# Local attention: the bias goes from two TensorE products to one VectorE addition, and the scores from a float32 product of 64 rows to two fp32r products of 128 rows

## What is computed

```python
    dist = jnp.arange(WINDOW)[:, None] + WINDOW - jnp.arange(2 * WINDOW)[None, :]
    swa_bias = rel_bias[t5_bucket(jnp.maximum(dist, 0))].transpose(2, 0, 1)
...
    s = jnp.einsum('bnqhgd,bnjhd->bnhgqj', qb, kb).astype(jnp.float32) * d ** -0.5
    s = s + bias.astype(jnp.float32).reshape(Hkv, G, W, 2 * W)
...
    s = jnp.where(valid[None, :, None, None], s, -jnp.inf)
    sink = jnp.broadcast_to(sinks.astype(jnp.float32).reshape(1, 1, Hkv, G, 1, 1),
                            s.shape[:-1] + (1,))
    p = jax.nn.softmax(jnp.concatenate([s, sink], axis=-1), axis=-1)[..., :-1]
    out = jnp.einsum('bnhgqj,bnjhd->bnqhgd', p.astype(v.dtype), vb)
```

## Time and profile before

| | |
|---|---|
| median of 3 runs | 1845.63 us (1845.04 to 1845.82) |
| the profiled execution | 1847.51 us, span 1845.7 us |
| mean granted TensorE clock of the span | 0.98 of full |
| TensorE busy | 1772.8 us, 96% |
| VectorE, ScalarE, GpSimd busy | 51%, 45%, 52% |
| DMA | 162.15 MB, mean 88 GB/s |

### The profile page before, as it was taken

One profiled execution on the slowest core, in us unless ns is written; L12 is line 12 of the kernel. 1 busy time (PEld: TensorE's weight loads), 2 busy tenths in 40 slices (PEclk: granted clock), 3 DMA queues, 4 the chain that ended last, 5 costly groups with the idle time before them and its releaser, 6 DMA issues. The chain is left out here.

```text
span 1845.7 us, 27645 instructions
## 1 busy us (share of the span) xinstructions
PE 1772.8 (96%) x10494; PEld 1551.0 (84%) x10494; DVE 941.2 (51%) x1590; ACT 825.5 (45%) x1649; POOL 954.7 (52%) x697
## 2 busy tenths in 40 slices
PE   6999999999998999999979999999899989999998
PEld 4998777778887998899868988888788779989996
DVE  2444233345446772475048337995323288717842
ACT  4223434323334652455236327885434356515643
POOL 2453322224443775577436417994463247747862
PEclk8999999999999999999989988999999989999999
DMA  6232121113352223233324312011251223333341
GB/s 226 80 92 58 44 60 41 55 44 97 89 182 80 87 97 115 80 115 109 120 66 127 114 34 69 2 36 58 92 160 60 78 69 92 109 109 92 93 137 46
DMA packets 222900, 162.15 MB, mean 88 GB/s; under 512 B 9768, under 2 KB 197296, under 8 KB 222768
## 3 DMA queue, kind: packets, MB, share of 16 engines
q1 hardware_dynamic: 221712, 159.32, 28.1%
q10 hardware_dynamic: 1056, 1.06, 0.2%
HBM read 156.15 MB, written 2.11 MB: 86 GB/s over the span
## 5 line engine op out<-in xcount | busy, mean ns | idle before, releaser
L350 POOL TENSOR_TENSOR w_low<-ring,w_high 128x1024 fp32r<-128x1024 f32 (+2 forms) x223 | 484.2, 2175 | 639.5 <-ACT w_high L342 639.3
L363 PE MATMUL psum<-hT,w_high 128*128 128x512 f32 (+1 forms) x1072 | 378.2, 353 | 9.9 <-PEq L185 6.4
L342 ACT ACTIVATE w_high<-ring 128x1024 fp32r<-128x1024 f32 (+2 forms) x223 | 212.2, 955 | 383.4 <-PE psum L365 383.4
L364 PE MATMUL psum<-hL,w_high 128*128 128x512 f32 (+1 forms) x1072 | 371.0, 346 | 0.0
L365 PE MATMUL psum<-hT,w_low 128*128 128x512 f32 (+1 forms) x1072 | 370.7, 346 | 0.0
L363 PEld LDWEIGHTS psum<-hT,w_high 128*128 128x128 f32 x1072 | 206.7, 193 | 38.3 <-issue 11.8
L365 PEld LDWEIGHTS psum<-hT,w_low 128*128 128x128 f32 x1072 | 206.1, 192 | 24.9
L364 PEld LDWEIGHTS psum<-hL,w_high 128*128 128x128 f32 x1072 | 206.8, 193 | 21.6
L1711 POOL TENSOR_TENSOR w_low<-ffn_sums,w_high 128x512 fp32r<-128x512 f32 x120 | 169.3, 1425 | 50.4 <-ACT w_high L1706 50.0
L1711 POOL TENSOR_TENSOR w_low<-ring,w_high 128x512 fp32r<-128x512 f32 x120 | 155.4, 1298 | 60.8 <-ACT w_high L1706 54.3
L363 PE MATMUL psum<-ffn_th,w_high 128*128 128x256 f32 x640 | 181.6, 284 | 5.0 <-DVE ffn_g L1945 3.4
(11 more groups left out here) (418 smaller groups left out, 3766.1 us busy)
## 6 DMA issues: line engine op xcount, KB each, us to landing
ring<-in_w_in SPq DMA_DIRECT2D x58, 512.0 KB, 3.4
ring<-in_ffn_w_up SPq DMA_DIRECT2D x44, 512.0 KB, 3.7
ring<-in_w_gate SPq DMA_DIRECT2D x22, 512.0 KB, 3.7
ring<-in_w_up SPq DMA_DIRECT2D x22, 512.0 KB, 4.7
ring<-in_w_down SPq DMA_DIRECT2D x20, 512.0 KB, 3.7
ring<-in_ffn_w_down SPq DMA_DIRECT2D x20, 512.0 KB, 3.8
ring<-in_nsa_w_in SPq DMA_DIRECT2D x18, 512.0 KB, 3.5
ring<-in_ca_wkv SPq DMA_DIRECT2D x16, 512.0 KB, 3.6
```

Of the source, the lines that this page charges most:

```text
L342: nc.scalar.activation(tile_view(w_high, n, SPLIT), tile_view(ring, n, RING), ACT.Copy).then_inc(w_hi, 1)
L350: nc.gpsimd.tensor_tensor(tile_view(w_low, n, SPLIT), tile_view(ring, n, RING), tile_view(w_high, n, SPLIT), ALU.subtract).then_inc(w_lo, 1)
L363: nc.tensor.matmul(ps, lhsT=sh, rhs=mh, start=first, stop=False)
L364: nc.tensor.matmul(ps, lhsT=sh, rhs=ml_, start=False, stop=False)
```

## The change

The bias is no longer multiplied on TensorE. Its row of 384 is made reversed by the constants; it comes back as `bias_back`, and VectorE copies it once with its columns turned over into `bias`, float32. In each step of the local attention VectorE copies the two heads' sinks into the last column of the pair's slots in `sprob`, waits for the scores, adds PSUM and bias into `sprob`, and takes the maximum from there. ScalarE's exponential reads and writes `sprob`.

For the scores, each query head has a tile `wq[h]` of 128 rows: its high part in the 64 rows of its key head, its low part in the other 64. For each key head `wk[g]` has the high part in both halves and `wkl[g]` the low part in both. Two fp32r products of 128 rows give (high + low) x high and (high + low) x low. The tiles `wq`, `wk` and `wkl` are written from the transposes in PSUM: high parts by ScalarE, low parts by VectorE, each piece 64 partitions x 512. `qkT` keeps four tiles. `put` has one buffer in place of two, and the reversed identity is gone from the constants. Other hunks, not shown, move tiles to other addresses and rename semaphores.

```diff
@@ -111,9 +110,9 @@
         if 0 <= dist[u] < 128:
-            c[bucket[u], C_OH + u] = 1
+            c[bucket[u], C_OH + 383 - u] = 1
         else:
-            c[BUCKETS, C_OH + u] = NEG
+            c[BUCKETS, C_OH + 383 - u] = NEG
     return np.concatenate([c, r], axis=1)
...
@@ -762,31 +764,36 @@
         norm_gain = at("anorm_gain", [P, D], 8192)
-        qkT = at("qkT", [P, 9, S], 18432)
+        qkT = at("qkT", [P, 4, S], 18432)
         sqr = at("sqr", [P, 54, HD], 18432)
...
-        raw = at("raw", [P, SWA_H, 256], 57344)
         rows = at("rows", [P, 2, S], 65536, F32R)
-        mcol = at("mcol", [P, 2, NT, ML_H], 69632)
-        toep = [at(f"toep{i}", [P, SWA_H, 258], 69760 + 8256 * i, F32R) for i in range(2)]
-        sinks = at("sinks", [P, SWA_H], 104704)
-        yswa = at("yswa", [P, NT, 512], 86272)
-        sprob = at("sprob", [P, 4, 258], 12288)
-        sprobT = at("sprobT", [P, 4, 256], 94464, F32R)
-        sprobL = at("sprobL", [P, 4, 256], 98560, F32R)
-        put = at("put", [P, 2, 2, P], 102656)
+        bias = at("bias", [P, SWA_H, 256], 69632)
+        bias_back = at("bias_back", [P, SWA_H, 256], 77824)
+        wq_at = [26624 + 2048 * i for i in range(5)] + [77824 + 2048 * i for i in range(3)]
+        wq = [at(f"wq{h}", [P, S], wq_at[h], F32R) for h in range(SWA_H)]
+        wk = [at(f"wk{g}", [P, S], (83968, 102400)[g], F32R) for g in range(2)]
+        wkl = [nc.alloc_sbuf_tensor_at(f"wkl{g}", [P, S], F32R, offset=x_at + (6 + g) * 4 * S) for g in range(2)]
+        yswa = at("yswa", [P, NT, 512], 86016)
+        sprob = at("sprob", [P, 4, 258], -32)
+        sprobT = at("sprobT", [P, 4, 256], 94208, F32R)
+        sprobL = at("sprobL", [P, 4, 256], 98304, F32R)
+        put = at("put", [P, 2, P], 104448)
         yfox = at("yfox", [P, NT, 256], 45056)
...
@@ -823,15 +830,13 @@
                 for h in (2 * hp, 2 * hp + 1):
-                    g, i = h // 4, h % 4
+                    g = h // 4
                     k0 = max(t - 1, 0)
                     nk = (t + 1 - k0) * P
-                    rows_g = slice(HD * g, HD * g + HD)
                     units.append({
                         "width": nk + 1,
-                        "scores": [(0, nk + 2, anti_r, toep[0][:, h, 256 - nk:258]),
-                                   (0, nk + 2, anti_r, toep[1][:, h, 256 - nk:258]),
-                                   (0, nk, qkT[rows_g, 4 + i, q_tile(t)], qkT[rows_g, 8, k0 * P:k0 * P + nk])],
+                        "scores": [(0, nk, wq[h][:, q_tile(t)], wk[g][:, k0 * P:k0 * P + nk]),
+                                   (0, nk, wq[h][:, q_tile(t)], wkl[g][:, k0 * P:k0 * P + nk])],
                         "keys": [(j * P, vswa[:, k0 + j, g, :]) for j in range(nk // P)]})
...
@@ -973,6 +978,13 @@
                 pe.wait_ge(out_a, NT * (c + 1) - sum(n_v[:c + 1]))
+        def wait_qk_out(pe, i):
+            if i >= 4:
+                pe.wait_ge(qk_v, i - 1)
+            else:
+                pe.wait_ge(qk_v if i % 2 == 0 else qk_a, i // 2 + 1)
 
...
@@ -1029,7 +1041,7 @@
                 if i >= 3:
-                    pe.wait_ge(qk_v if (i - 3) % 2 == 0 else qk_a, (i - 3) // 2 + 1)
+                    wait_qk_out(pe, i - 3)
                 for t in range(NT):
...
@@ -1230,6 +1242,18 @@
                 scaled(False, qkT[:, i, :], bank[5 + i % 3], qk_gain(i)).then_inc(qk_a, 1)
+            def window_high(i):
+                a.wait_ge(turned_qk, i + 1)
+                src, gain = bank[5 + i % 3], qk_gain(i)
+                for g in range(2):
+                    if i < 8:
+                        nc.scalar.activation(wq[4 * g + i - 4][part(g), :], src[part(g), :], ACT.Copy,
+                                             scale=gain[part(g), :]).then_inc(w_high_qk, 1)
+                    else:
+                        for e in range(2):
+                            nc.scalar.activation(wk[g][part(e), :], src[part(g), :], ACT.Copy,
+                                                 scale=gain[part(g), :]).then_inc(w_high_qk, 1)
 
...
@@ -1244,9 +1268,12 @@
             qk_out(3)
-            qk_out(5)
+            window_high(4)
+            window_high(5)
             split_high(a, feat0 + 4 + SPLIT)
-            qk_out(7)
+            window_high(6)
+            window_high(7)
+            window_high(8)
             feature_out(5)
...
@@ -1300,7 +1327,8 @@
                         a.wait_ge(turned, v_ - 3)
-                    nc.scalar.activation(pairs[s]["prob"][:, v_ % 4, 0:wd], bank[S0 + b][:, 0:wd], ACT.Exp,
+                    src = sprob[:, v_ % 4, 0:wd] if s < n_swa else bank[S0 + b][:, 0:wd]
+                    nc.scalar.activation(pairs[s]["prob"][:, v_ % 4, 0:wd], src, ACT.Exp,
                                          bias=npeak[s % 2][:, b:b + 1], accum_out=p_total[s % 4][:, b:b + 1]).then_inc(exped, 1)
...
@@ -1337,17 +1365,6 @@
 
-            def toeplitz():
-                v.wait_ge(raw_in, 32)
-                sink = sinks[:, :].unsqueeze(2)
-                nc.vector.tensor_copy(toep[0][:, :, 0:256], raw[:, :, :]).then_inc(toep_high, 1)
-                nc.vector.tensor_copy(toep[0][:, :, 256:257], sink).then_inc(toep_high, 1)
-                for part_ in toep:
-                    nc.vector.tensor_scalar(part_[:, :, 257:258], sink, 0.0, None, ALU.mult)
-                v.wait_ge(toep_high, 2)
-                nc.vector.tensor_tensor(toep[1][:, :, 0:256], raw[:, :, :], toep[0][:, :, 0:256], ALU.subtract)
-                nc.vector.tensor_tensor(toep[1][:, :, 256:257], sink, toep[0][:, :, 256:257], ALU.subtract).then_inc(toeped, 1)
             def split_columns():
...
@@ -1360,7 +1377,9 @@
                 if c == 0:
-                    toeplitz()
+                    v.wait_ge(bias_in, 32)
+                    nc.vector.tensor_copy(bias[:, :, :], bias_back[:, :, ::-1])
                 if c == 1:
...
@@ -1390,6 +1409,16 @@
 
+            def window_low(i):
+                src, gain = bank[5 + i % 3], qk_gain(i)
+                v.wait_ge(w_high_qk, 2 * (i - 3) if i < 8 else 12)
+                for g in range(2):
+                    high = wq[4 * g + i - 4] if i < 8 else wk[g]
+                    for low in [wq[4 * g + i - 4][part(1 - g), :]] if i < 8 else [wkl[g][part(e), :] for e in range(2)]:
+                        ins = nc.vector.scalar_tensor_tensor(low, src[part(g), :], gain[part(g), :], high[part(g), :],
+                                                             ALU.mult, ALU.subtract)
+                ins.then_inc(qk_v, 1)
             def log_rows():
...
@@ -1425,10 +1454,12 @@
             qk_out(2)
-            qk_out(4)
+            window_low(4)
+            window_low(5)
             feature_out(4)
-            qk_out(6)
-            qk_out(8)
+            window_low(6)
+            window_low(7)
+            window_low(8)
             convolve()
...
@@ -1471,7 +1502,18 @@
                 merge.upto(slices_after_step(s - 1))
-                if s < n_pairs:
+                if s < n_swa:
+                    wd = pairs[s]["units"][0]["width"]
+                    h0, to = 2 * s % SWA_H, sprob[:, 2 * (s % 2):2 * (s % 2) + 2, :]
+                    if s >= 2:
+                        v.wait_ge(turned, 2 * s - 2)
+                    link(nc.vector.tensor_copy(to[:, :, wd - 1:wd], sinks[:, h0:h0 + 2].unsqueeze(2)))
+                    v.wait_ge(scored, s + 1)
+                    link(nc.vector.tensor_tensor(to[:, :, 0:wd - 1], psum[:, S0:S0 + 2, 0:wd - 1],
+                                                 bias[:, h0:h0 + 2, 257 - wd:256], ALU.add))
+                    nc.vector.tensor_reduce(npeak[s % 2], to[:, :, 0:wd], AXX, ALU.max, negate=True).then_inc(peaked, 1)
+                elif s < n_pairs:
                     wd = pairs[s]["units"][0]["width"]
...
@@ -1490,9 +1532,9 @@
                     v.wait_ge(summed, 2 * p + 2)
-                    if p >= 2:
-                        v.wait_ge(collected, p - 1)
-                    nc.vector.tensor_tensor(put[:, p % 2, :, :], bank[V0][:, 0:2 * P].rearrange("p (b c) -> p b c", c=P),
+                    if p >= 1:
+                        v.wait_ge(collected, p)
+                    nc.vector.tensor_tensor(put[:, :, :], bank[V0][:, 0:2 * P].rearrange("p (b c) -> p b c", c=P),
                                             by[p % 2].unsqueeze(2).to_broadcast([P, 2, P]), ALU.mult).then_inc(divided, 1)
```

More of the change, by code:

```diff
@@ L48 @@
 BUCKETS = 32
-ARENA = 104736
+ARENA = 105472
 NSA_ARENA = 104192
@@ L73 @@
 C_END = C_OH + 384
-R_ID, R_ANTI, R_MQ, R_MT, R_SEL = 0, P, 2 * P, 3 * P, 4 * P
+R_ID, R_MQ, R_MT, R_SEL = 0, P, 2 * P, 3 * P
 R_END = R_SEL + 4 * P
@@ L195, in build @@
         stat = sb("stat", [P, 160])
+        mcol = sb("mcol", [P, 2, NT, ML_H])
+        sinks = sb("sinks", [P, SWA_H])
         sb("pad", [P, (-nc.sbuf_base) % 2048 // 4])
@@ L209, in build @@
         const_r = sb("const_r", [P, R_END], dt=F32R)
```

(41 more changed lines are left out.)

13 lines of the change are left out of this document (6 added, 7 removed).

## The result

The changed kernel takes 1823.87 us (median of 4 runs, 1822.74 to 1824.9); the kernel before, in the same comparison, 1845.36 (4 runs, 1845.04 to 1845.82). The ratio is 0.9882, 95% interval [0.9868, 0.9895]: faster by 1.2%. Forecast were 1821.7 and a range of 1817.5 to 1829. The profiled execution took 1822.74 us, span 1821.0, against 1847.51 and 1845.7.

What follows compares the result with a forecast made beforehand. TensorE was taken to bound the sixteen local-attention pairs: 24.2 us saved there, less 0.5 for sink copies, plus 0.2 at the start, 23.9 in all. From 1845.6 that gives 1821.7 us, range 1817.5 to 1829.

Steps and rivals of the forecast that it cites:

- TensorE is the bound, and its work is the saving: Sixteen local-attention pairs, 184 to 278 us: TensorE work taken out shortens the span one for one, 24.2 us saved.
- The addition is covered: Local attention: VectorE's bias addition before the maximum, 0.74 us with its wait, costs nothing behind merge and value products.
- The margin: Local attention: time left in VectorE's chain after the addition, 1.4 us per wide pair and 1.1 per narrow.
- if it took twice as long, it would still be covered: Local attention: VectorE's bias addition would cost nothing even at double its length.
- The sink copy: Local attention: VectorE copies held by GpSimd cost 0.5 us, bounds 0 and 12; rival of frequent holding, 1833 us, chance 8%.
- The queries' and keys' pieces: At 147 to 163 us: convolution starts 1.3 us later, 2.4 us in hand, so zero cost; otherwise up to 1 us.
- The start: Kernel start: the constants' transfer shrinks by 64 KB, 0.2 us gained, down to 0.
- The rival of 2 to 5 us by half-clock stretches: Behind the local attention: a half-clock stretch may come or go, 1817 or 1826 us; chance 15%, half each side.
- products of 0.21: Local attention scores: each new product costs 0.21 us, giving 1826 us; chance 12%.
- VectorE's chain as the bound: Local attention: held addition and maximum bound each step, slower than before at 1849 us; chance 3%.
- a stage that isn't shortened: Local attention: split weights bound it and TensorE's busy time is only filled up, about 1845 us; chance 2%.

Runs made afterwards that it cites:

- Run 3: Changed kernel with each local-attention pair's score products issued twice, 64 more products: 1828.62 us, ratio 0.9904 to the kernel before.
- run 2: Changed kernel keeping VectorE's bias addition, but scores from one float32 product of 64 rows per head: 1832.76 us, ratio 0.9936 to the kernel before.
- run 4: Changed kernel without the sixteen sink copies and bias additions, maximum and exponential reading PSUM: 1823.4 us, ratio 0.9879 to the kernel before.
- run 6: Changed kernel with each VectorE bias addition issued four times: 1839.04 us, ratio 0.9955 to the kernel before.
- run 5: Changed kernel with each VectorE bias addition issued twice: 1822.91 us, ratio 0.9867 to the kernel before.
- run 7: Changed kernel with VectorE's sink copy moved behind the wait for the scores: 1826.51 us, ratio 0.9886 to the kernel before.
- Run 1: Changed kernel again, no edit, beside new runs of the kernel before: 1822.34 us, ratio 0.9875.
- run 8: Changed kernel with each low part of the keys written three times, eight more VectorE pieces before the convolution: 1828.15 us, ratio 0.9896 to the kernel before.

## Why the prediction was right, and where it was not

- **TensorE is the bound, and its work is the saving.** Right. 24.2 us were predicted, and 24.3 came in the stage by the shift; 1.64 worked out and 1.65 measured per wide pair, 1.13 and 1.1 per narrow. The step that carried it was to price by start-to-start distances and to count the slow neighbours of a change of type (0.34 us to the next start behind the float32 scores, where 0.23 is usual). Run 3 shows the price of a product, run 2 how the sum divides.
- **The addition is covered.** Right: run 4 puts it at 0.00. The addition with its wait takes 0.72 (226.84 to 227.56) of the 0.74 worked out, of which 0.05, for the wait, stood in no row; behind the addition's 0.69 are 0.03. The margin was mis-sized. Predicted were 1.4 us. By the rows of the changed kernel, the second sum is read 2.81 us behind the scores' end (226.57 to 229.38), not 1.86 + 0.74 = 2.60, since the addition starts 0.27 behind that end where the maximum started 0.11; and the distance to the next transposes is 3.65, not 3.78: 0.11 of it is the slow follower of the old scores, which the prediction counted as saved and yet kept in this distance. 3.65 + 0.18 - 2.81 = 1.02, and run 6 gives 0.95. It was also priced at one pair; the step of 203.49 has 0.5, as run 5 shows. The very first pair has only 0.4, but there the exponential waits for ScalarE's own table load (1.28 us, from 184.33), so a later addition costs nothing: run 5 lost nothing in it. The claim "if it took twice as long, it would still be covered" missed by 0.42 us.
- **The sink copy.** The mechanism was right, the 0.5 us too much: one copy in sixteen was held, 1.81 us, to 0.03 behind the subtraction's end, and ended before the scores did. That it costs nothing is owed to its place: run 7 pays 4.3 us for the same copy one line later.
- **The queries' and keys' pieces.** The starts came out within 0.3 us, partly by luck: ScalarE's last piece ended 0.4 earlier than worked out (159.5 for 159.9), and VectorE's four took 3.04 us, not 2.76. The cost is nothing, and 1.3 to 1.4 us were in hand in place of 2.4. The low part was done 0.4 later than worked out (175.8 for 175.4), and TensorE came to the tile at 177.13 instead of 177.84: 0.2 because the row read for it is VectorE's copy, which in the kernel before starts 0.2 behind TensorE's product, and 0.5 by what had been gained before: a gain ahead of a stage takes from the margin of what that stage waits for.
- **The start.** The shift is 0.2 at 28 us, as said, but this isn't shown to be the smaller transfer: the eight runs, which start as the changed kernel does, lie from -0.56 to +0.26 us against it there. The transfer itself (`const_in`, 512 KB before and 448 now) took 8.2 us to landing in both. That transfers run side by side there the trace of the kernel before shows: `anorm_gain` was issued at 2.58 us and took 7.7 to landing, `const_in` was issued at 3.75.
- **The waits of 1.4 and 0.5 us behind the stage** change nothing: the kernel before has the same two, and the shift is 24.8 both before and behind them. The prediction looked at waits only up to 300 us, and so never saw them.
- **Clock.** The predicted time is 2.2 us below the median. The sum was 0.9 too small (23.9 for 24.8 between the profiled executions): 0.5 for a sink copy that cost nothing, 0.3 at 30 us, 0.1 in the stage. The other 3.0 lie between profiled executions and medians: I took the before's median to lie 1.9 under its profiled execution, and the changed kernel's lies 1.1 above its own. Run 1 shows what this scatter is. The rival of 2 to 5 us by half-clock stretches thus holds for both kernels: over 32 us of the same part the clock is 0.79 or 0.89 in two runs of the changed one (run 1), and whole executions of the kernel before have 0.980 to 0.984 and 1842.33 to 1847.54 us. The medians of this comparison differ by 21.5 us, those of run 1's group by 23.4, the profiled executions by 24.8; runs 4 and 5, whose edits cost 0.0 and 0.4 us in the stage, lie 22.4 and 24.5 under the kernel before. Whether the missing 1 to 3 are chance or a lasting cost of more half-clock in the changed kernel stays open.

The rivals that fell: the sink copy (run 7 shows when it would have held), products of 0.21 (run 3), VectorE's chain as the bound (run 6 shows that even three additions more leave it faster than before), and a stage that isn't shortened.

## What to carry over

Where an engine is busy to the last tenth of a microsecond, price an edit on it by the distances between starts, the neighbours included, and expect it in the span one for one, as long as all else arrives in time (run 3: 7.5 us expected, 7.57 lost). For the work that moves to an engine with idle time, work out the margin at every step of the loop and take the least, with the start delay of the new first instruction; test it by doubling the work, since free work says nothing about how near the edge is. And put small SBUF-to-SBUF copies on VectorE ahead of a wait, where being held by GpSimd falls into idle time: the 1.81 us of the one held here cost nothing there, and one line later the copies cost 4.3 us (run 7).

## What the hardware showed that I had not expected

- A copy need not be large to be held: 2 elements per partition took up to 2.15 us (run 7), where 0.17 is usual.
- Turning the columns over cost nothing that shows. The copy of 2048 columns with the source read backwards takes 1.22 us, and the kernel before's cast of as many columns, read forward (L1343), took 1.22 too:

```profile
51.25 1.22 DVE L1382 COPY bias<-bias_back 128x2048 f32<-128x2048 f32 x1
```

- The same short waits of TensorE, with the same instructions around them, were followed by half clock in four runs and not in the others. Behind the waits of 1.4 and 0.5 us at 285 to 288 us the changed kernel kept full clock, while run 5, with the same two waits, lost 1.6 us there; runs 2, 4 and 7 lost 1.4 to 1.6 too, the kernel before and runs 1, 3, 6 and 8 nothing. Over the 10 us with these waits the mean granted clock is 0.83 in runs 2, 4, 5 and 7 and 1.00 in the rest. The stretch in the changed kernel and in run 5:

```profile
283.00:293.00 10.00, 8.09 (x41) 5.51 (x40) 2.56 (x6) 3.78 (x10) 1.75 (x2) 1.00 0.09 26
```
```profile
283.00:293.00 10.00, 8.10 (x34) 5.29 (x33) 1.79 (x4) 3.67 (x9) 1.74 (x2) 0.83 0.09 26
```
